# Two 256-column matmuls of an expert unit joined into one of 512 columns, with the two results added on VectorE

## The reference, cut to what matters

```python
q = (x @ w_q)                       # 8 heads, two halves of 128
s = einsum(q, sub_keys)             # 128 scores for each half, 16 best of each, 16 best of the 256 pairs
g = softmax(top_v)                  # weight of each picked expert
a = gelu(einsum('td,thkd->thk', x, u[experts]))
y = einsum('thk,thkd->td', g * a, v[experts])
```

## Time and profile before

| | us |
|---|---|
| median of 3 runs | 1457.29 (1457.16 to 1457.70) |
| the profiled execution, its own time | 1455.16 |
| its span, first to last instruction | 1453.4 |
| TensorE busy (matmuls) | 1379.7 |
| VectorE busy | 949.6 |
| ScalarE busy | 775.3 |
| GpSimd busy | 458.7 |

### The profile page before, as it was taken

How to read it: one execution, slowest core, us unless ns; L and a number is a source line. 1 busy time by engine, 2 the same in 40 slices (tenths; PEclk the granted TensorE clock), 3 DMA queues, 4 the chain that set the end, 5 groups by cost and what they waited for, 6 DMA issues and landing times.

```text
span 1453.4 us, 22196 instructions
## 1 busy us (share of the span) xinstructions
PE 1379.7 (95%) x8932; PEld 1251.2 (86%) x8932; DVE 949.6 (65%) x1510; ACT 775.3 (53%) x1251; POOL 458.7 (32%) x247
## 2 busy tenths in 40 slices
PE   6999899999986999799799999999999999999997
PEld 6898789999865777799799999988888888888886
DVE  5676777887788756498976666555465555555555
ACT  5465745444444355445379999544454444545443
POOL 1530013545363101688742221111211211221113
PEclk9999999999997999999999999999999999999999
DMA  7553256777885822557555445566666566666665
GB/s 237 172 151 95 94 173 216 257 242 255 273 283 188 308 88 87 189 160 210 175 157 156 145 146 155 194 202 211 214 207 203 188 212 216 205 203 199 199 214 195
DMA packets 190325, 278.86 MB, mean 192 GB/s; under 512 B 9184, under 2 KB 120544, under 8 KB 189968
## 3 DMA queue, kind: packets, MB, share of 16 engines
q1 hardware_dynamic: 184640, 266.19, 56.2%
q10 hardware_dynamic: 5184, 10.02, 1.8%
q0 software_dynamic: 400, 1.25, 0.3%
HBM read 266.41 MB, written 11.01 MB: 191 GB/s over the span
## 4 chain that ended last, share of the span: by engine, by line
PE 60%; DVE 6%; DMA 1%; ACT 1%; POOL 1%; issue 1%; DVEq 0%; SPq 0%; ACTq 0%
PE bank L679 16%; PE bank L646 16%; PE bank L684 8%; PE bank L651 8%; PE bank L946 4%; PE bank L619 3%; PE bank L623 1%; PE bank L864 1%; PE bank L883 1%; DMA sb_raw<-w_in 1%; DVE sb_lo L1344 1%; DMA sb_raw<-peer_uT 1%; PE bank L871 1%; PE bank L905 1%; ACT sb_hi L980 0%
## 5 line engine op out<-in xcount | busy, mean ns | idle before, releaser
L1970 POOL TENSOR_TENSOR sb_lo<-sb_raw,sb_hi 128x1024 fp32r<-128x1024 f32 x149 | 378.6, 2548 | 821.3 <-ACT sb_hi L980 821.1
L980 ACT ACTIVATE sb_hi<-sb_raw 128x1024 fp32r<-128x1024 f32 (+2 forms) x427 | 443.1, 1048 | 269.6 <-DMA sb_raw<-peer_v 68.4
L1344 DVE TENSOR_TENSOR sb_lo<-sb_raw,sb_hi 128x1024 fp32r<-128x1024 f32 (+2 forms) x279 | 391.2, 1413 | 234.0 <-ACT sb_hi L980 232.5
L646 PE MATMUL bank<-sb_act_hi,sb_hi 128*128 128x256 f32 x1632 | 407.7, 288 | 8.2 <-ACT sb_hi L980 7.1
L646 PE MATMUL bank<-sb_act_lo,sb_hi 128*128 128x256 f32 x1632 | 402.2, 284 | 0.0
L646 PEld LDWEIGHTS bank<-sb_act_hi,sb_hi 128*128 128x128 f32 x1632 | 314.4, 193 | 11.0 <-ACT sb_hi L980 5.0
L646 PEld LDWEIGHTS bank<-sb_act_lo,sb_hi 128*128 128x128 f32 x1632 | 315.2, 193 | 1.5
L679 PE MATMUL bank<-sb_hi,sb_hid_hi 128*128 128x512 f32 x600 | 234.2, 390 | 0.9 <-DVE sb_hid_lo L1659 0.9
L651 PE MATMUL bank<-sb_act_hi,sb_lo 128*128 128x256 f32 x1632 | 230.0, 284 | 4.8 <-POOL sb_lo L1970 4.7
L679 PE MATMUL bank<-sb_hi,sb_hid_lo 128*128 128x512 f32 x600 | 234.4, 391 | 0.0
L651 PEld LDWEIGHTS bank<-sb_act_hi,sb_lo 128*128 128x128 f32 x1632 | 210.7, 192 | 5.8 <-POOL sb_lo L1970 5.8
(11 more groups left out here) (329 smaller groups left out, 1445.0 us busy)
## 6 DMA issues: line engine op xcount, KB each, us to landing
sb_raw<-peer_uT SPq DMA_DIRECT2D x128, 512.0 KB, 3.9
sb_raw<-peer_v SPq DMA_DIRECT2D x128, 512.0 KB, 4.9
sb_raw<-w_in SPq DMA_DIRECT2D x52, 512.0 KB, 4.7
sb_ada_w<-ada_wT SPq DMA_DIRECT2D x48, 512.0 KB, 5.6
sb_raw<-w_gate SPq DMA_DIRECT2D x22, 512.0 KB, 3.8
sb_raw<-w_up SPq DMA_DIRECT2D x22, 512.0 KB, 3.6
sb_raw<-w_down SPq DMA_DIRECT2D x22, 512.0 KB, 3.9
sb_raw<-w_out SPq DMA_DIRECT2D x16, 512.0 KB, 3.6
```

Of the source, the lines that this page charges most:

```text
L646: e.matmul(bank[:, j * T:(j + 1) * T], hi[:, k, j * P:(j + 1) * P], part[:, k0 + k, :], start=i == first_i and j == 0 and k == 0 and part ...
L980: e.activation(flat_of(i, "hi"), flat_of(i, "raw"), ACT.Copy).then_inc(hi_done[i % R], 1)
L1344: e.tensor_tensor(flat_of(i, "lo"), flat_of(i, "raw"), flat_of(i, "hi").bitcast(F32), ALU.subtract).then_inc(lo_done[i % R], 1)
L1970: e.tensor_tensor(flat_of(i, "lo"), flat_of(i, "raw"), flat_of(i, "hi").bitcast(F32), ALU.subtract).then_inc(lo_done[i % R], 1)
```

## The change

The tokens' hi and lo, which lay next to each other already, are now one tensor `act_words`, and `act_both[:, chunk]` is a view of 2 x 256 words of it, hi and then lo. The new `unit_panel` replaces `feature_panel` for units 11 to 63. For each half j it takes a bank of its own; a weight piece's hi is stood once and 512 columns, hi and lo of the tokens, are moved past it, so that the bank's left half gathers hi x hi and its right half hi x lo; the weights' lo goes onto the left half with 256 columns as before. So a block is 8 matmuls of 512 columns and 8 of 256, and the right half must be added to the left.

VectorE does this with two instructions for each bank: it copies the right half to SBUF and adds the left. Beside G (`sum_halves`, at `SUM_LATER` = 5 steps after the b) the sum goes back into the bank, and ScalarE's `early_out` comes at `UNIT_LATER` = 6 steps after the b, with a gelu for each half. In the main loop the sum goes to `hid_raw`, and ScalarE's gelu works there in place.

```diff
-    G=0, act_hi=32768, act_lo=34816, ring=36864, hid=36864 + 5 * 2048, const=50176, cols=50840, mod=50968, stat=51024, pick_T=51520,
+    G=0, act_hi=32768, act_lo=34816, ring=36864, hid=36864 + 5 * 2048, const=50176, cols=50840, mod=50968, stat=51024, pick_T=51520, addend=52800,
...
-G_LATER = 5
+G_LATER, SUM_LATER, UNIT_LATER = 5, 5, 6
...
+        beside_G = [u for what, u, b in expert_matrix_order() if what == "u" and b == 1]
+        unit_summed = Events(sem("unit_summed"), [(u, j) for u in beside_G for j in range(2)])
+        unit_gelu = Events(sem("unit_gelu"), [(u,) for u in UNIT_ORDER if u >= EARLY])
...
-        act_T = pair("act", DC)
+        act_words = place("act", 2 * DC * T, F32R, OFF["act_hi"])
+        act_T = Pair(by_chunk(act_words[:, 0:DC * T]), by_chunk(act_words[:, DC * T:2 * DC * T]))
+        act_both = act_words.rearrange("p (w c t) -> p c w t", w=2, c=DC)
+        addend = place("addend", T)
...
+            def unit_panel(u, ready):
+
+                key = ("uT", u)
+                bank = [take(key, j) for j in range(2)]
+                k0 = 0
+                for i in span[key]:
+                    hi, lo, kb = cut_of(i, "hi"), cut_of(i, "lo"), plan[i].kc
+                    first, last = i == span[key][0], i == span[key][-1]
+                    pe.wait_ge(*hi_of(i))
+                    for j in range(2):
+                        for k in range(kb):
+                            pe.wait_ge(*ready[k0 + k])
+                            e.matmul(bank[j][:, :].rearrange("p (w t) -> p w t", w=2), hi[:, k, j * P:(j + 1) * P], act_both[:, k0 + k],
+                                     start=first and k == 0, stop=False, skip_group_check=True)
+                    pe.wait_ge(*lo_of(i))
+                    for j in range(2):
+                        for k in range(kb):
+                            ins = e.matmul(bank[j][:, 0:T], lo[:, k, j * P:(j + 1) * P], act_T.hi[:, k0 + k, :],
+                                           start=False, stop=last and k == kb - 1, skip_group_check=True)
+                        if last:
+                            ins.then_inc(*fills(key, j))
+                    k0 += kb
+                    if not last:
+                        ins.then_inc(*frees(i))
+                        yield
+                release[span[key][-1]] = [full(key, 1)]
+                for j in range(2):
+                    give(key, j)
...
-                        early_panel = feature_panel(("uT", n), act_T, h2)
+                        early_panel = unit_panel(n, h2)
...
-                    whole(feature_panel(("uT", UNIT_ORDER[at]), act_T, h2))
+                    whole(unit_panel(UNIT_ORDER[at], h2))
...
-                act.wait_ge(*full(("uT", u)))
-                e.activation(by_chunk(early_buf[b]), by_chunk(psum(("uT", u))[:, :]), ACT.Gelu).then_inc(*gives(("uT", u)))
-                act.wait_ge(*freed(("uT", u)))
+                if u < EARLY_BESIDE_SELECT:
+                    act.wait_ge(*full(("uT", u)))
+                    e.activation(by_chunk(early_buf[b]), by_chunk(psum(("uT", u))[:, :]), ACT.Gelu).then_inc(*gives(("uT", u)))
+                    act.wait_ge(*freed(("uT", u)))
+                else:
+                    for j in range(2):
+                        act.wait_ge(*unit_summed.at(u, j))
+                        e.activation(early_buf[b][:, j * T:(j + 1) * T], psum(("uT", u), j)[:, 0:T], ACT.Gelu).then_inc(*gives(("uT", u), j))
+                    for j in range(2):
+                        act.wait_ge(*freed(("uT", u), j))
...
-            for at in range(len(order) + G_LATER):
+            for at in range(len(order) + UNIT_LATER):
...
-                if at >= G_LATER:
+                if G_LATER <= at < len(order) + G_LATER:
...
-                    elif b == 1:
+                if at >= UNIT_LATER:
+                    what, n, b = order[at - UNIT_LATER]
+                    if what == "u" and b == 1:
...
-                        if at >= HID_BUFS:
-                            act.wait_ge(*hid_used["peer", at - HID_BUFS])
-                        act.wait_ge(*full(("uT", u)))
-                        e.activation(hid_raw[i], by_chunk(psum(("uT", u))[:, :]), ACT.Gelu).then_inc(*gives(("uT", u)))
+                        for j in range(2):
+                            act.wait_ge(*freed(("uT", u), j))
+                        e.activation(hid_raw[i], hid_raw[i], ACT.Gelu).then_inc(*unit_gelu.inc(u))
...
-            for what, n, b in expert_matrix_order():
+            def sum_halves(u):
+                for j in range(2):
+                    bank = psum(("uT", u), j)
+                    dve.wait_ge(*full(("uT", u), j))
+                    own(e.tensor_copy(addend, bank[:, T:2 * T]))
+                    e.tensor_tensor(bank[:, 0:T], bank[:, 0:T], addend, ALU.add).then_inc(*unit_summed.inc(u, j))
+                    dve.wait_ge(*unit_summed.at(u, j))
+
+            order = list(expert_matrix_order())
+            for at, (what, n, b) in enumerate(order + [("", 0, 0)] * SUM_LATER):
+                if at >= SUM_LATER and order[at - SUM_LATER][0] == "u" and order[at - SUM_LATER][2] == 1:
+                    sum_halves(order[at - SUM_LATER][1])
...
-                        dve.wait_ge(*freed(("uT", u)))
+                        if at >= HID_BUFS:
+                            dve.wait_ge(*hid_used["peer", at - HID_BUFS])
+                        for j in range(2):
+                            bank, h = psum(("uT", u), j), hid_raw[i][:, j, :]
+                            dve.wait_ge(*full(("uT", u), j))
+                            own(e.tensor_copy(h, bank[:, T:2 * T]))
+                            e.tensor_tensor(h, bank[:, 0:T], h, ALU.add).then_inc(*gives(("uT", u), j))
+                        dve.wait_ge(*unit_gelu.at(u))
```

2 lines of the change are left out of this document (1 added, 1 removed).

## The result

The changed kernel takes 1463.87 us (median of 8 runs, 1459.49 to 1465.87) against 1457.22 (8 runs, 1454.58 to 1458.72): a ratio of 1.004, 95% interval 1.0028 to 1.0051. It is slower by 6.7 us. Forecast were 1461.8, +4.5.

A forecast was written before the change was run, and what follows sets the result against it. TensorE, busy 95% of the span, was taken as the bound. Main loop -6.8 + 0.3, recurring beside G +4.7, start +4.9 and end +1.4 sum to +4.5 us: 1461.8 us on the runs' scale, range 1449 to 1470.

The forecast's parts named there:

- A block gains 0.107 us: Both stages: a block of 8 512-column and 8 256-column matmuls takes 2.773 us on TensorE, 0.107 less.
- The rival that the pair keeps its old pace: Both stages: a joined matmul takes 2 x 0.120 us, so the gain is gone, +15.8, 1473 us; chance 0.08.
- Main loop -6.5: Main loop: 64 blocks gain 0.107 us each, -6.8, and the first round is allowed a wait of 0.3.
- No wait in the steady round: Main loop: gate multiplication comes 2.5 us later, but the next hi is still ready with a margin of 1.6 us.
- The start +4.9: Beside G, up to step 14: TensorE idle 4.7 us at step 5, then half clock and a second wait; +4.9 us.
- Six G's at 0.95 and six a's at 0.45: Beside G, steps 14 to 106: recurring TensorE waits for banks that ScalarE frees late, +8.4 us in six rounds.
- The walk through `idle_banks`: Beside G: following bank takes through the step list shows those that come ahead of, or in, the ScalarE step freeing them.
- The rival that ScalarE's lead covers them: Beside G: ScalarE is 1.9 us ahead instead of 1.1, so no recurring waits; -3.9, 1453.4 us; chance 0.20.
- the one that no bank is waited for: Beside G, start included: no waits for banks, all 106 blocks gain, -11.3, 1446.0 us; chance 0.06.
- The end +1.4: Ahead of the main loop: its first unit waits for the two banks of unit 31's halves; +1.4 us.
- The sums beside G at nothing: Beside G: VectorE's 1.7 us sum for each unit is covered by its idle third, so costed at nothing.
- The VectorE rival: Beside G: VectorE becomes the bound, ScalarE waits for matrices; +8 us on top, 1470 us; chance 0.12.

The follow-up runs named there:

- e8: Joined matmuls in the main loop only, plus four more 128x256 copies per unit on VectorE there, against the kernel before: 1484.25 us, 1.019.
- e6: The changed kernel, but units 11 and 12 by the old panel in one bank each: 1462.29 us, 1.0047 of before.
- e3: Against the changed kernel: beside G two banks per unit, but 256-column matmuls and no sums; main loop as before: 1467.63 us, 1.0073 of before.
- e2: The changed kernel with joined matmuls beside G only, main loop as before the change: 1469.59 us, 1.0084 of before.
- e5: The changed kernel without VectorE's copies and adds beside G, so hi x lo is missing from units 11 to 31: 1460.77 us, 1.003 of before.
- e12: The changed kernel with each sum beside G moved behind the step's own work on VectorE: 1461.84 us, 1.003 of before.
- e4: The changed kernel with G_LATER, SUM_LATER, UNIT_LATER = 3, 3, 4 in place of 5, 5, 6: 1467.33 us, 1.0074 of before.
- e7: The changed kernel, but beside G only even units joined with two banks, odd ones by the old one-bank panel: 1453.84 us, 0.9978 of before.
- e9: Against e7 (every second unit beside G joined): no VectorE sums beside G, so hi x lo is missing from even units there: 1452.49 us, 0.9966 of before.
- e10: Against e7 (every second unit beside G joined): each sum put behind the step's own work on VectorE: 1450.28 us, 0.9951 of before.
- e11: Against e10 (alternate units joined, sums behind): one-bank units put out at step + 5 as before the change: 1450.51 us, 0.9951 of before.
- e1: The changed kernel with joined matmuls in the main loop only, units beside G as before with one bank each: 1449.69 us, 0.9953 of before.

## Why the prediction was right where it was, and where not

- **A block gains 0.107 us.** The mechanism held, the term was too large: 0.096 in the loop, 0.075 beside G. Over both stages this is the largest part of what the sum is short of, 64 x 0.011 + 1.1 = 1.8 us. The pace was read from the product with v, where 512-column matmuls follow each other; behind 256-column ones eight of them need 0.03 more. That the moved operand lies in two places costs nothing: 1.81 for eight, and eight of the product with v take 8 x 0.2267 = 1.81. The rival that the pair keeps its old pace is out. The Trainium skill (TensorE: Matmul & The Clock Gate, Back-to-back issue gap) would have given the loop's 64 blocks 1.3 us, as an estimate from its figures for 256 and 512 columns, which it states for an isolated matmul; measured were 6.1.
- **Main loop -6.5.** It was -5.2: 0.7 by the size of the block's gain (64 x 0.011), 0.6 by waits that happen once (0.9 for 0.3). "No wait in the steady round" held. The margin behind it was mis-sized, 1.6 forecast and 0.7 by e8. The trace shows one reason: the prediction began the sums when the matmuls end, and VectorE is then in a lo that is held up by GpSimd's, until 2.3 us later. It did no harm here.
- **The start +4.9.** It was +5.0 (step 14 began at 757.96 before, not at 758.03). The pause forecast at 4.7 was 4.78 and the clock was at half behind it. e6 shows that the pause comes of the two banks of the first units, e3 that it needs neither joined matmuls nor sums.
- **Six G's at 0.95 and six a's at 0.45.** They were 5.30 for 5.7 and 2.45 in five for 2.7. The walk through `idle_banks` named all the places where TensorE waited, and one (the a at step 65) where it didn't. e3 shows that the banks make those of the G's without faster blocks or sums; those of the a's are 1.35 us there, about half. The rival that ScalarE's lead covers them is out, and with it the one that no bank is waited for.
- **The end +1.4.** It was 1.44 of idle time, 1.7 from start to start.
- **The sums beside G at nothing.** This is the step whose mechanism failed: "I take it that the idle third covers it". The sign that the prediction named for this, waits of TensorE for matrices, is there: 1.52 us in two behind step 14. Among the kernels with two banks for every unit, those with the sums ahead of the matrices have such waits (2 in the change, 5 in e2), and so has e6, with two banks for all but the first two units (4 in all); those without sums (e3, e5) or with the sums behind (e12) have none. Leaving the sums out or putting them behind gives back 2.2 and 2.0 us from step 14 on, and 2.6 and 2.0 by medians. Each of these alone is within the scatter; they agree, and about 2 us is what they say. A third of VectorE's time idle doesn't cover a sum that stands ahead of the matrices: VectorE reaches it before TensorE has filled the bank, waits, then sums, and the matrices behind are late (the rows at 847.29 to 855.82, and e4). The VectorE rival was right in the mechanism and, at 8 us for about 2, some four times too large. With one bank for every second unit (e7, e9 to e11) the same effect isn't told from scatter by the traces.

Added up: the loop 1.3 us short, the blocks beside G 1.1 (3.7 forecast, 2.6 found), the waits for matrices 0.7 (1.52 less the 0.84 that the kernel before loses there itself), the end 0.3, the start 0.1, less 0.4 + 0.25 where the waits for banks were smaller: +4.5 becomes +7.4 by the traces, +6.7 by the medians. Two traces of the same stage can differ by 3.4 us (the change and e2), so how near the forecast came is in part luck; that the start, the recurring waits and the end came each at its place and size is not.

Why e1 gains 7.6 us in its medians where its loop gives 5.3 stays open; so does why the same instructions take 2.2 us more beside G in e8 than in e1, and 3.4 more in e2 than in the change.

## What to carry to other kernels

When an edit makes a worker hold one more of a few buffers that go round, walk the list of takes and gives and note for each take how many steps it is ahead of or behind the one that frees it; here that named all the places, and put 9.8 us on those that recur and the one at the end, where 9.4 were measured. The banks and what goes with them took 12.0 us (e3), and the faster matmuls of that stage gave about 3.2. Ask of a new instruction what stands behind it in its engine's queue: if it waits on another engine, it also costs the lead that its own engine had, as in e4, where VectorE stood still 44.6 us. Before a difference of a few us in one stage is given a cause, look at two kernels that run the same instructions there; here they differed by 2.2 and 3.4 us. Splitting a change by stage shows what to keep: the joined matmuls in the main loop alone are 0.9953 of the time before.
